# Three reorderings in a one-core transformer and state-space kernel: a weight split ahead of a chunk's chain, skip products later, attention scores inside a projection

## The reference, cut to what matters

```python
def dilated_attention_mixer(h, w_qkv, w_out, rel_bias):
    qkv = (h @ w_qkv).reshape(bsz, seq, 3, N_HEADS, HEAD_DIM)      # 16 heads of 64
    ...
    return o.reshape(bsz, seq, D_MODEL).astype(h.dtype) @ w_out

def ssd_scan(xh, dt, a, bm, cm):                 # chunks of 128 tokens, 8 groups of 4 heads
    def step(state, inp):
        cum = jnp.cumsum(lac, axis=1)
        decay = jnp.exp(jnp.where(causal, cum[:, :, None] - cum[:, None], -jnp.inf))
        xdt = xc * dtc[..., None]
        cb = jnp.einsum('blgn,bsgn->blsg', cc, bc)
        y = jnp.einsum('blsgr,bsgrp->blgrp', cb[..., None] * decay, xdt)
        y = y + jnp.einsum('blgn,bgrpn->blgrp', cc, state) * jnp.exp(cum)[..., None]
    ...
def ssd_mixer(...):
    y = (ssd_scan(xh, ...) + rev(ssd_scan(rev(xh), ...))
         + xh * d_skip.astype(f32)[:, None])     # the skip products
    y = y.reshape(bsz, seq, D_INNER) * jax.nn.silu(z.astype(f32))
```

## Time and profile before

| | |
|---|---|
| median of 3 runs | 2120.02 us (2118.34 to 2122.9) |
| the profiled execution | 2118.97 us, of which its span is 2116.9 us |
| PE busy | 2044.0 us, 97% of the span |
| POOL busy | 1046.8 us, 49% |
| DVE, ACT busy | 923.7 us, 838.0 us |

### The profile page before, as it was taken

The page is one execution under the profiler, slowest core; times in us unless marked ns, Lnnn a source line. Parts: engine busy times, 40 slices in busy tenths (PEclk is TensorE's granted clock), DMA queues, the critical chain, the costliest instruction groups (busy, mean ns, idle before and its releaser), DMA issues.

```text
span 2116.9 us, 27293 instructions
## 1 busy us (share of the span) xinstructions
PE 2044.0 (97%) x10588; PEld 1702.4 (80%) x10588; DVE 923.7 (44%) x1425; ACT 838.0 (40%) x1349; POOL 1046.8 (49%) x855
## 2 busy tenths in 40 slices
PE   8999999999999999999999989999979999999998
PEld 6878888888787777888888768888877878888886
DVE  3184433321233343433323678888873214434221
ACT  4123222222244443222233376666673235553442
POOL 4444555545533224545455387888873432323342
PEclk9999999999999999999999989999989999999999
DMA  4223232233432213332233333343422331112131
GB/s 163 89 90 110 94 98 87 94 91 101 123 90 80 74 57 100 100 100 83 90 97 104 93 100 103 107 127 104 123 76 70 93 101 61 46 63 72 54 86 60
DMA packets 267034, 193.37 MB, mean 91 GB/s; under 512 B 9443, under 2 KB 263703, under 8 KB 266920
## 3 DMA queue, kind: packets, MB, share of 16 engines
q1 hardware_dynamic: 264380, 191.20, 30.0%
q10 hardware_dynamic: 2540, 0.56, 0.1%
HBM read 189.46 MB, written 2.27 MB: 91 GB/s over the span
## 4 chain that ended last, share of the span: by engine, by line
PE 50%; issue 24%; POOL 17%; ACT 5%; DVE 3%; POOLq 0%; ACTq 0%; DVEq 0%
POOL wlo L601 17%; PE bank L1851 15%; PE bank L1853 15%; PE bank L1852 15%; PE bank L2412 1%; ACT whi L679 1%; PE bank L2275 1%; PE bank L2428 1%; PE bank L2271 1%; ACT ybuf L947 0%; ACT bank L937 0%; ACT L954 0%; PE bank L2426 0%; PE bank L2386 0%; PE bank L2373 0%
## 5 line engine op out<-in xcount | busy, mean ns | idle before, releaser
L601 POOL TENSOR_TENSOR wlo<-raw,whi 128x512 fp32r<-128x512 f32 (+1 forms) x668 | 859.2, 1317 | 980.5 <-ACT whi L679 980.5
L1851 PE MATMUL bank<-hHi,whi 128*128 128x512 f32 x1408 | 557.7, 396 | 15.1 <-POOL wlo L601 10.3
L1853 PE MATMUL bank<-hHi,wlo 128*128 128x512 f32 x1408 | 549.5, 390 | 0.0
L1852 PE MATMUL bank<-hLo,whi 128*128 128x512 f32 x1408 | 549.2, 390 | 0.0
L679 ACT ACTIVATE whi<-raw 128x2048 fp32r<-128x2048 f32 (+1 forms) x168 | 303.7, 1808 | 456.7 <-PE bank L1853 451.8
L1851 PEld LDWEIGHTS bank<-hHi,whi 128*128 128x128 f32 x1408 | 264.8, 188 | 76.8 <-POOL wlo L601 12.4
L1853 PEld LDWEIGHTS bank<-hHi,wlo 128*128 128x128 f32 x1408 | 264.9, 188 | 56.4
L1852 PEld LDWEIGHTS bank<-hLo,whi 128*128 128x128 f32 x1408 | 265.1, 188 | 55.0 <-issue 1.2
L1851 PE MATMUL bank<-whi,hHi 128*128 128x256 f32 x896 | 264.4, 295 | 6.4 <-ACT gO L1179 3.7
L1852 PE MATMUL bank<-wlo,hHi 128*128 128x256 f32 x896 | 255.3, 285 | 0.0
L1853 PE MATMUL bank<-whi,hLo 128*128 128x256 f32 x896 | 255.3, 285 | 0.0
(11 more groups left out here) (334 smaller groups left out, 2925.2 us busy)
## 6 DMA issues: line engine op xcount, KB each, us to landing
raw<-in_ssd_w_in SPq DMA_DIRECT2D x48, 512.0 KB, 4.9
raw<-in_ffn_w_gate SPq DMA_DIRECT2D x44, 512.0 KB, 4.4
raw<-in_ffn_w_up SPq DMA_DIRECT2D x44, 512.0 KB, 4.5
raw<-in_gla_w_in SPq DMA_DIRECT2D x40, 512.0 KB, 4.4
rows<-cums SPq DMA_DIRECT2D x64, 256.0 KB, 5.3
raw<-in_conv_w_in SPq DMA_DIRECT2D x24, 512.0 KB, 4.4
raw<-in_ffn_w_down SPq DMA_DIRECT2D x32, 384.0 KB, 3.5
raw<-in_attn_w_qkv SPq DMA_DIRECT2D x24, 512.0 KB, 4.5
```

Of the source, the lines that this page charges most:

```text
L601: ins = pool.tensor_tensor(wlo[s][:, part], raw[s][:, part], whi[s][:, part].bitcast(F32), ALU.subtract)
L1851: pe.matmul(dst, hi1, hi2, start=first, stop=False)
L1852: pe.matmul(dst, hi1, lo2, start=False, stop=False)
L1853: return pe.matmul(dst, lo1, hi2, start=False, stop=last)
```

## The change

In an SSD group POOL's `unit_low` of the B/C unit moves from behind `coupled(4g)` to ahead of it (all groups but 1 and 7). On ACT `skips(g)` moves from ahead of the `high` of the B/C unit to behind the `high` of the z unit, some eleven rows later (all groups but 7). In the attention the first two parts of the scores are issued in the middle of the first projection piece, for pairs 1 to 7; `out_part(0, range(6))` of the last pair becomes two calls of three slices, with the second `turn_rows` between them.

```diff
                         pool.tensor_tensor(h4(xw_buf(step, d)), h4(chunk("xt", c)), bc(heads("wst", c, d, g), 64),
                                            ALU.mult).then_inc(S("xw_ready"), 1)
-                coupled(NT * g)
                 if g != 1 and more:
                     unit_low(UNIT_OF["z", max(g - 1, 0)] + 2)
+                coupled(NT * g)
                 coupled(NT * g + 1)
...
                         group_root(g - 1)
-                    skips(g)
+                    if not more:
+                        skips(g)
                     if g != 1:
                         unit_high(UNIT_OF["z", max(g - 1, 0)] + 2)
                     exponential(NT * g)
...
                     if more:
                         unit_high(UNIT_OF["x", g + 1] + 2)
+                        skips(g)
                     if g:
                         turned_out(g - 1, 1)
...
                     if kind == "tv":
-                        mark(tokens(u % 2, e, bank[at % 2]))
+                        mark(tokens(u % 2, e, bank[at % 2], between))
                     else:
-                        mark(chan(bank[at % 2][:, :], u % 2, pair(e), hHi, hLo, range(KT)))
+                        chan(bank[at % 2][:, :], u % 2, pair(e), hHi, hLo, range(4), True, False)
+                        if between:
+                            between()
+                        mark(chan(bank[at % 2][:, :], u % 2, pair(e), hHi, hLo, range(4, KT), False, True))
...
                 for p in range(PAIRS):
+                    def early_scores():
+                        scores(p, 0)
+                        scores(p, 1)
+
+                    projected(attn_piece(p, 0), early_scores if p else None)
                     if p == 0:
-                        projected(attn_piece(p, 0))
-                    scores(p, 0)
-                    scores(p, 1)
-                    if p:
-                        projected(attn_piece(p, 0))
+                        early_scores()
                     scores(p, 2)
...
                         pe.wait_ge(S("v_ready"), 4 * 3 + 2)
-                        out_part(0, range(6))
+                        out_part(0, range(3))
                     if p:
                         turn_rows(p - 1, 1)
-                    projected(attn_piece(p, 2))
+                    if p < PAIRS - 1:
+                        projected(attn_piece(p, 2))
+                    else:
+                        out_part(0, range(3, 6))
                     if p:
                         weigh(p - 1)
```

More of the change, by code:

```diff
@@ L2021, in _, with projected @@
                 qk = m_att["qk"]
-                def projected(at):
-                    if at is None:
-                        return
+                def projected(at, between=None):
                     kind, i, e = ATT_PIECES[at]
```

## The result

The changed kernel takes 2098.25 us, the median of four runs (2096.86 to 2098.94), against 2120.37 (2118.34 to 2122.9) for the kernel before in the same comparison: ratio 0.9894, interval 0.9877 to 0.9911. That is 22.1 us less.

The account below looks back on a forecast made before the run. It took PE, busy 97% of the span, as the bound. Groups 2 to 6 (8.8), group 0 (0.8), clock (1.6) and attention (3.3) summed to 14.5 us less, 2105.5 against the median of 2120.02; range 2101.5 to 2111.0.

Parts of the forecast that it names:

- No wait of PE for wlo in groups 2 to 6: Sign of being right, in the SSD groups: PE no longer waits for the low part of the weights.
- (a): Rival: attention gives nothing, changes of kind or a wait at part 2 eat 4.0 us; time 2108.8; chance 0.14.
- (b): Rival: SSD gain given back within the group, PE waiting for MT or taps; time 2116.7; chance 0.07.
- (c): Rival: the split, now first, holds up the chunk's chain while ACT's `high` is late; slower, 2124; chance 0.04.
- Rival (d): More gain: group 0's whole 1.47, changes of kind free, one more half-clock stretch gone; 2101.6; chance 0.11.
- The wait of 1.76 us goes whole: SSD groups 2 to 6: PE's wait for the B/C split vanishes in each, 8.8 us for five groups.
- Attention, 3.3: Attention's term: 4.0 us from six waits, less 1.4 for changes of kind, plus 0.7 in the last pair.
- six waits go: 4.0 us: Attention, pairs 2 to 7: PE's wait of 0.66 us for the split of `weigh`'s result vanishes in each.
- The price of a split: Attention: each projection split by scores adds changes of kind on PE, 0.20 us, in seven pairs 1.4 us.
- My upper bound, 4.9: Attention's largest gain in us, if changes of kind are free; the lower bound was 1.9.
- Group 0, 0.8 within 0 and 1.47: SSD group 0: PE's 1.47 us wait for the split goes, against POOL's full load; the middle, 0.8 us, taken.
- Clock, 1.6 within 0 and 1.7: Half-clock stretch behind group 5's wait, costing 1.7 us of matmul time, goes with that wait; 1.6 us gained.

Follow-up runs that it names:

- e14_only_2_to_6: Kernel before, with POOL's B/C split ahead of the first chunk's chain in groups 2 to 6 alone: 2109.21 us, ratio 0.9949.
- e2: Kernel before plus POOL's new order alone, skips where they were, attention as before: 2101.79 us, ratio 0.992.
- e4: Kernel before plus POOL's and ACT's new orders, attention as before: 2101.69 us, ratio 0.992.
- e5: Changed kernel with `out_part` of the last pair in one call of six slices again: 2096.85 us, ratio 0.9897.
- e7: Changed kernel with the two early parts of the scores at two places of the projection piece, two slices apart: 2099.61 us, ratio 0.991.
- e13: Kernel before, with POOL's B/C split ahead of the first chunk's chain in group 0 alone: 2113.85 us, ratio 0.9975.
- e1: Kernel before plus the attention's part of the change alone, SSD groups in their old order: 2114.37 us, ratio 0.9979.
- e11_wait_back: Changed kernel plus a PE wait for the first MT ahead of the third projection piece in groups 2 to 6: 2109.06 us, ratio 0.9953.
- e6_group0: Changed kernel with group 0 in the old order, first chunk's chain ahead of the split: 2103.45 us, ratio 0.9925.
- e3_skips: Kernel before plus ACT's new order alone, skips later, POOL's order as before: 2112.66 us, ratio 0.9975.

## Why the prediction was too small

**Right.** What it names for groups 2 to 6 and for the attention's waits happened. No wait of PE for wlo in groups 2 to 6, none for `oLo`, none of `weigh` for pT in the last pair. POOL began the split 1.28 us after xw (forecast 1.2) and took 5.00 (5.03); MT had 3.95 us of room (4.1); the skips cost nothing. The distance of two groups came out at 45.36 where 45.6 was forecast. Of the rivals, (a), (b) and (c) fell: the attention gave 5.2, no wait for MT or taps came up in a middle group, and the split ended 3.8 us ahead of PE. Rival (d) came nearest in time, 2101.6, but only in part by its terms: group 0 gave more than the 1.47 it put there and the clock more than 1.6 beyond the forecast, while the changes of kind were not free.

**"The wait of 1.76 us goes whole", 8.8 for five groups.** It went, but it was worth 2.03. PE's way from the second L2253 to L2271 in group 3 took 1381.28 - 1373.30 = 7.98 us before (the earlier trace rows has its end; the L2253 row is below) and takes 1370.57 - 1364.63 = 5.94 now.

```profile
1373.30 0.60 PE L2253 MATMUL bank<-ident,szs 128*128 128x128 f32 x4
```

The step that failed is the equation of a wait's price with its listed idle. The listed idle begins where that row's modelled end lies, at 1373.90. But where nothing holds PE, the next matmul starts before that end: in the changed kernel 0.36 us after the row's start, not 0.60. The 0.24 belong to the wait. The other 0.04 are the first products behind a wait, which run a little slower. Five groups: 10.2 us, 1.4 over the term; e14_only_2_to_6 has 11.0 at equal clock (0.6 uncertain).

**Attention, 3.3.** The same error in "six waits go: 4.0 us": 0.66 listed, 0.93 worth, 5.6 in all. The price of a split was 0.25 and not 0.20. One pair, from `weigh` to `weigh`, was 688.38 - 663.33 = 25.05 and is 685.83 - 661.46 = 24.37, and every other pair 24.3: 0.71 on average, six times 4.3, and the last pair 0.9 on top. That makes the 5.2 measured. My upper bound, 4.9, was set by free splits and not by a dearer wait. Pairs 0 and 1, with one split and no wait to lose, came out even (51.12 us to the first `weigh`, and 51.09).

**Group 0, 0.8 within 0 and 1.47.** Here the step was wrong and not only the size. I bounded the gain by the wait that goes, with POOL's load against it. The load did take all of it back, at MT. But PE's last wait in the group is not for POOL, it is for a bank that DVE frees, and DVE's chain starts with PE's projection piece. I had both rows in front of me and took them for a reason to expect something between nothing and 1.47, where they showed another chain with a 3.33 us wait at its end: 2.4 us, above my upper bound. The earlier DVE chain did not pay for it either: its two additions took 1.89 us and not 2.52. By the rule of the Trainium skill (SBUF — State Buffer, "SBUF: two separate sides"), that a DVE instruction with two SBUF inputs and a GpSimd one that reads SBUF take one port pair in turn, the prediction estimated 0.1 for this term. The trace agrees with the rule in that one such addition takes 0.43 us with no POOL instruction beside it (1394.85 in the changed kernel) and up to 1.40 us beside POOL's instructions in both kernels. It does not bear out that the earlier chain loses by it.

**Clock, 1.6 within 0 and 1.7.** The stretch behind group 5's wait went, as put. That I took its own price for the upper bound was wrong: the mean loss over the runs fell by 3.5 us (0.7 uncertain). The kernels with PE's waits gone both in group 0 and in groups 2 to 6 (e2, e4, e5, e7 and the change) lose 17.8 to 19.1; those that keep them in both or in one lose 20.8 (e13) to 23.1 (e1), and e11_wait_back, with five waits put back, 22.3. In the profiles groups 0 and 1 together took 88.8 to 91.7 us in the old order, the dearer ones with a window like that of e6_group0 above, and 86.2 to 87.5 in the new. One kernel does not fit: e3_skips keeps all the waits, those of groups 2 to 6 0.4 us shorter, and lost only 19.2. That waits of this size raise the clock's loss is made likely by e11_wait_back, which changes nothing else, and not shown: the rise of 3.2 us is little more than the 2.4 us between the two measurements of the changed kernel itself. Which of the waits bring such stretches stays open.

**The sum.** Attention 5.2, group 0 and 1 2.7, groups 2 to 6 10.2: 18.1 of the 19.2 at equal clock are accounted for by distances in the trace, and 3.5 are the clock's. Of the 7.6 us missing in the forecast, 3.3 come from the groups 2 to 6 (1.4) and the attention (1.9), and of these 3.0 from listed idle taken as the price of a wait, 1.4 in the five groups and 1.6 in the six pairs; 1.9 come from groups 0 and 1, 1.9 from the clock; the rest is within what the two measurements differ by. The measured time lies 3.25 us below the range. Its lower end was made of single terms of 0.7 to 1.6 us, while the error in a wait's price went the same way in eleven waits at once, and groups 0 and 1 and the clock each went beyond their bounds.

## What to carry to other kernels

On an engine whose matmuls overlap, price a wait from start to start: the distance between two fixed instructions with the wait, less the same distance elsewhere without it; the listed idle was 0.22 to 0.28 us short here in each wait. When a wait goes in a stretch with several, follow what its end started on the other engines (here DVE's chain) to the last wait of the stretch: the gain is set there, and may be smaller or larger than the wait itself. With differences below half a per cent, compare at the same mean granted clock, or take a dozen runs: e5_tail_whole leaves out a part worth 0.9 us and had a lower median than the first measurement of the whole change.

## What the runs showed of the hardware

- The lower clock's cost is not fixed by the program. 51 runs of one kernel had mean clocks of 0.986 to 0.992 and times of 2113 to 2125 us, and the time follows the clock. In the changed kernel, which lacks thirteen PE waits of 0.66 to 1.8 us and the one of 3.33, the mean loss was 19.1 instead of 22.6 us; with five of 1.5 us put in it was 22.3. That the waits are the cause is likely and not shown: e3_skips keeps them all and lost 19.2.
- Scores wedged into a running accumulation of a projection cost 0.25 us for one place (one pair, read from rows) and 0.40 more for a second (seven pairs of e7_kinds), half of that because two parts side by side overlap by 0.20.
- The idle time listed ahead of a matmul was short of what the wait cost: 1.76 listed and 2.04 from start to start in group 3, 0.66 and 0.93 in the attention, 1.52 and 1.74 in e11_wait_back.
- The two additions of 256 columns late in DVE's chain in group 0 took 2.52 us in the kernel before and 1.89 in the changed one, beside POOL's instructions in both. One such addition with no POOL instruction beside it took 0.43 us.
